# Block two's recurrent mixer in another order: convolution and gate products before the dense gate branch, its functions grouped over all heads

## The reference, cut to what matters

```
def recurrent_mixer(h, ...):
    gate_branch = gelu(h @ w_y + b_y)
    xr = h @ w_in + b_in
    xr = causal_depthwise_conv_2(xr, conv_w, conv_b)       # width 4
    gate_r = sigmoid(block_diag(xr, w_a) + b_a)            # 4 heads of 256 x 256
    gate_i = sigmoid(block_diag(xr, w_x) + b_x)
    log_a = 8.0 * gate_r * log_sigmoid(lam)
    a, mult = exp(log_a), sqrt(-expm1(2.0 * log_a))
    h_t = a_t * h_{t-1} + mult_t * gate_i_t * xr_t         # over the 512 tokens
    return (h * gate_branch) @ w_out + b_out
```

## Time and profile before

| what | value |
|---|---|
| median of 3 runs | 2665.47 us (2664.84 to 2668.5) |
| the profiled execution | 2664.44 us |
| its span, first to last instruction | 2662.4 us |
| granted TensorE clock, mean | 0.942 |
| PE busy | 2396.6 us, 90% |
| DVE busy | 1375.9 us, 52% |
| ACT busy | 1017.8 us, 38% |

### The profile page before, as it was taken

One profiled execution on the slowest core, in us unless ns is written; L12 is line 12 of the kernel. 1 busy time (PEld: TensorE's weight loads), 2 busy tenths in 40 slices (PEclk: granted clock), 3 DMA queues, 4 the chain that ended last, 5 costly groups with the idle time before them and its releaser, 6 DMA issues.

```text
span 2662.4 us, 35555 instructions
## 1 busy us (share of the span) xinstructions
PE 2396.6 (90%) x13228; PEld 1916.8 (72%) x13228; DVE 1375.9 (52%) x1960; ACT 1017.8 (38%) x1543; POOL 308.6 (12%) x250
## 2 busy tenths in 40 slices
PE   8996689999999996689999997948999993799998
PEld 6774567888877774667888886736888883688886
DVE  3546656656544546655656544545443345434433
ACT  5534334323234544324423235374332233423323
POOL 0032312000031032312000021011000013100001
PEclk9998699999999999699999998978999996899999
DMA  4210003555432210003555431211222221122222
GB/s 153 72 63 9 2 27 126 195 184 196 135 111 68 75 60 12 2 18 118 194 189 193 144 105 54 87 40 64 95 95 95 95 95 39 48 95 95 95 95 87
DMA packets 68648, 247.68 MB, mean 93 GB/s; under 512 B 7616, under 2 KB 8128, under 8 KB 68544
## 3 DMA queue, kind: packets, MB, share of 16 engines
q1 hardware_dynamic: 68544, 246.26, 27.8%
HBM read 244.13 MB, written 2.10 MB: 92 GB/s over the span
## 4 chain that ended last, share of the span: by engine, by line
PE 79%; DVE 10%; ACT 5%; issue 3%; POOL 1%; DMA 0%; SPq 0%; DVEq 0%; ACTq 0%; POOLq 0%
PE dense L532 23%; PE dense L533 22%; PE dense L534 22%; PE aux L769 1%; PE aux L630 1%; DVE outer L1987 1%; DVE inv L1989 1%; PE aux L937 1%; PE aux L740 1%; PE aux L756 1%; PE aux L637 1%; ACT wh L1146 1%; DVE nt L1758 1%; PE aux L532 1%; PE aux L747 1%
## 5 line engine op out<-in xcount | busy, mean ns | idle before, releaser
L532 PE MATMUL dense<-xh,wh 128*128 128x512 f32 x1904 | 757.1, 398 | 52.3 <-DVE xl L1732 25.6
L1146 ACT ACTIVATE wh<-raw 128x1024 fp32r<-128x1024 f32 x342 | 362.4, 1060 | 1030.3 <-PE dense L534 1016.5
L533 PE MATMUL dense<-xl,wh 128*128 128x512 f32 x1904 | 745.8, 392 | 0.0
L534 PE MATMUL dense<-xh,wl 128*128 128x512 f32 x1904 | 745.2, 391 | 0.0
L1700 DVE TENSOR_TENSOR wl<-raw,wh 128x1024 fp32r<-128x1024 f32 x342 | 419.1, 1225 | 573.7 <-ACT wh L1146 572.2
L532 PEld LDWEIGHTS dense<-xh,wh 128*128 128x128 f32 x1904 | 360.2, 189 | 152.9 <-DVE xl L1732 39.9
L534 PEld LDWEIGHTS dense<-xh,wl 128*128 128x128 f32 x1904 | 359.9, 189 | 76.5
L533 PEld LDWEIGHTS dense<-xl,wh 128*128 128x128 f32 x1904 | 360.1, 189 | 73.8 <-issue 1.7
L532 PE MATMUL dense<-hidh,wh 128*128 128x512 f32 x864 | 342.4, 396 | 1.9 <-DVE hidl L1732 1.9
L534 PE MATMUL dense<-hidh,wl 128*128 128x512 f32 x864 | 341.7, 396 | 0.0
L533 PE MATMUL dense<-hidl,wh 128*128 128x512 f32 x864 | 341.7, 395 | 0.0
(11 more groups left out here) (328 smaller groups left out, 2482.5 us busy)
## 6 DMA issues: line engine op xcount, KB each, us to landing
raw<-stream SPq DMA_DIRECT2D x362, 512.0 KB, 3.3
mraw<-mod_stream SPq DMA_DIRECT2D x96, 512.0 KB, 4.2
x<-x_t SPq DMA_DIRECT2D x4, 512.0 KB, 7.4
y_t<-x SPq DMA_DIRECT2D x8, 256.0 KB, 2.1
cst<-consts SPq DMA_DIRECT2D x1, 993.0 KB, 10.3
cond<-c_rows SPq DMA_DIRECT2D x1, 512.0 KB, 11.5
pv_next<-vecs SPq DMA_DIRECT2D x3, 82.5 KB, 4.5
pv<-vecs SPq DMA_DIRECT2D x1, 116.0 KB, 10.7
```

The source lines that it names most:

```text
L532: pe.matmul(o, a, h, start=first, stop=False)
L533: pe.matmul(o, a, l, start=False, stop=False)
L534: return pe.matmul(o, b, h, start=False, stop=last)
L1146: act.activation(wh[:, slot].rearrange("p k m -> p (k m)"), raw[:, slot, :], ACT.Copy).then_inc(hi_done, 1)
```

## The change

The stream's order becomes C_IN (8), C_AX (4), C_Y (8), C_OUT (8).

- PE: `arriving` runs over C_IN; the head products use all six `aux` banks in turn, and the n-th of the 16 outputs waits only for the sigmoid of output n - 6; then C_Y; then C_OUT from `hidh` and `hidl` in place of `xh` and `xl`, so that `xh`, `xl` keep the mixer's input for C_Y.
- ACT: conv inputs as before, then all sigmoids and tanh of the four heads, then the 8 exp with the 8 squares, the 8 square roots, the 8 gelus with the rounding of the 8 outputs. The conversions of C_Y's and C_OUT's chunks stand at fixed places between them.
- DVE: for C_Y's first four chunks it copies the raw bank to `gate` (`gate_raw`), and Gelu is done later in place; the rest of the gates come from the bank. Scans of tile m, the product with the gate, and the low part follow, with the chunk conversions between them.
- `ga`, `gx` and `tb` hold all eight tiles, in buffers that are free then.

The rest (counts of semaphores shifted by 8, `triple` and `paired` that take their operands as arguments) follows from these. The core of the diff:

```
-C_Y, C_IN, C_AX, C_OUT, C_F0 = 0, 8, 16, 20, 28
+C_IN, C_AX, C_Y, C_OUT, C_F0 = 0, 8, 12, 20, 28
...
             norm_sums(4)
-            arriving(pl, C_Y, 6, 16, in_turn(xl_ready, XL2))
+            arriving(pl, C_IN, 6, KT, in_turn(xl_ready, XL2))
             for h in range(4):
                 pe.wait_ge(lo_done, pl.chunk(C_AX + h) + 1)
                 pe.wait_ge(hidl_ready, H0 + 2 * h + 2)
-                if h:
-                    pe.wait_ge(ax_read, 4 * h)
                 for o in range(4):
+                    n = 4 * h + o
+                    if n >= 6:
+                        pe.wait_ge(ax_read, n - 5)
                     for k in range(2):
-                        m = split_product(aux[o][:], (h % 2, (2 * o + k) * P), slice(0, P),
+                        m = split_product(aux[n % 6][:], (h % 2, (2 * o + k) * P), slice(0, P),
                                           (hidh[:, 2 * h + k, :], hidl[:, 2 * h + k, :]),
                                           k == 0, k == 1)
-                m.then_inc(pe_chunk, 1)
-            arriving(pl, C_OUT, 7, KT, in_turn(xl_ready, XL2 + 8))
+                    m.then_inc(pe_chunk if o == 3 else ax_pe, 1)
+            section(pl, C_Y, KT, xh, xl)
+            arriving(pl, C_OUT, 7, KT, in_turn(hidl_ready, H0 + 8), range(KT), hidh, hidl)
...
+            def gates(h):
+                for o in range(4):
+                    m, to = 2 * h + o % 2, (ga, gx)[o // 2]
+                    if o < 3:
+                        act.wait_ge(ax_pe, 3 * h + o + 1)
                     else:
+                        done(pl, C_AX + h)
+                    act.activation(to[m], aux[(4 * h + o) % 6][:], ACT.Sigmoid,
+                                   bias=vec2(("b_a", "b_x")[o // 2], m)).then_inc(ax_read, 1)
+            def tanhs(h):
+                act.wait_ge(ax_read, 4 * h + 2)
+                for m in (2 * h, 2 * h + 1):
+                    act.activation(tb[m], ga[m], ACT.Tanh, scale=small[:, 7, m:m + 1])\
+                       .then_inc(th_ready, 1)
...
+            for h in range(4):
                 gates(h)
+                tanhs(h)
+            for m in range(4):
+                decays(m)
+                if m:
+                    decay_square(m - 1)
+            done(pl, C_Y)
+            for m in range(4, KT):
+                decays(m)
+                decay_square(m - 1)
+            decay_square(KT - 1)
+            done(pl, C_Y + 1)
+            for m in range(KT):
+                root(m)
+            done(pl, C_Y, 1)
+            gelu(0)
+            gelu(1)
+            done(pl, C_Y + 1, 1)
+            gelu(2)
+            gelu(3)
+            for m in range(4, KT):
+                done(pl, C_Y + m % 2, m // 2)
+                gelu(m)
+                if m < 7:
+                    gated_hi_2(2 * (m - 4))
+                    gated_hi_2(2 * (m - 4) + 1)
+            gated_hi_2(6)
+            gated_hi_2(7)
...
+            def gate_raw(m):
+                i, j = m // 2, m % 2
+                dve.wait_ge(pe_chunk, pl.chunk(C_Y + j, i) + 1)
+                dve.tensor_copy(gate[:, m, :], dbank[j][:]).then_inc(bank_free[j], 1)
+                refill(pl, C_Y + j, i)
...
+            for m in range(3):
+                one_minus_a2(m)
+            gate_raw(0)
+            for m in range(3, KT):
+                one_minus_a2(m)
+            gate_raw(1)
+            for m in range(2):
+                scan(m)
+            gate_raw(2)
+            for m in range(2, 4):
+                scan(m)
+            gate_raw(3)
+            for m in range(4, KT):
+                scan(m)
+                if m == 5:
+                    refill(pl, C_Y, 2)
+                    gated(0)
+                    gated(1)
+            refill(pl, C_Y + 1, 2)
+            gated(2)
+            gated(3)
+            gated_lo(0)
+            gated_lo(1)
+            refill(pl, C_Y, 3)
+            gated(4)
+            gated(5)
+            gated_lo(2)
+            gated_lo(3)
+            refill(pl, C_Y + 1, 3)
+            gated(6)
+            gated(7)
+            for m in range(4, KT):
+                gated_lo(m)
```

More of the change, by code:

```diff
@@ L547, in dense, with triple @@
                 m.then_inc(pe_chunk, 1)
[L549 removed]
+            def triple(s, k, h=xh, l=xl):
                 slot = s % 2
@@ L575, in shared_low, with paired @@
                 return wait
-            def paired(pl, s, q, tile, order):
+            def paired(pl, s, q, tile, order, h=xh, l=xl):
                 done = []
@@ L1534, in _, with conv_input @@
             modulated(4, lambda m: small[:, 4, m:m + 1], lambda m: mod[:, 0, m:m + 1])
-            early(pl, C_Y, 6)
-            for i in range(4):
-                for j in range(2):
-                    m = i * 2 + j
-                    if i == 0:
-                        rest(pl, C_Y + j)
-                    else:
-                        done(pl, C_Y + j, i)
+            def conv_input(i, j):
+                m = i * 2 + j
+                act.wait_ge(xc_ready, m)
+                act.wait_ge(ua_zero, DEPTH + 1)
+                act.activation(ua[:, 3:S + 3], dbank[j][:], ACT.Identity,
+                               bias=vec2("b_in", m)).then_inc(bank_free[j], 1)
+                act.wait_ge(xc_ready, m + 1)
+                act.activation(hidh[:, m, :], xc[:, m, :], ACT.Copy).then_inc(hidh_ready, 1)
@@ new lines, in root, with gelu @@
+            def root(m):
+                act.wait_ge(m2_ready, m + 1)
+                act.activation(tb[m], tb[m], ACT.Sqrt).then_inc(m_ready, 1)
+            def gelu(m):
+                i, j = m // 2, m % 2
+                if m < 4:
+                    act.wait_ge(bank_free[j], pl.use(C_Y + j, i) + 1)
+                    act.activation(gate[:, m, :], gate[:, m, :], ACT.Gelu_apprx_tanh,
+                                   bias=vec2("b_y", m)).then_inc(gate_ready, 1)
+                else:
@@ L1543, in _ @@
                     act.activation(gate[:, m, :], dbank[j][:], ACT.Gelu_apprx_tanh,
                                    bias=vec2("b_y", m)).then_inc(bank_free[j], 1)
[L1545 to L1593, removed]
-                gates(h)
-                roots(h - 1)
@@ L1596, in _, with gated_hi_2 @@
-            roots(3)
+            def gated_hi_2(m):
+                act.wait_ge(h_ready, m + 1)
+                act.activation(hidh[:, m, :], xc[:, m, :], ACT.Copy).then_inc(hidh_ready, 1)
+            for h in range(4):
+                gates(h)
+                tanhs(h)
[7 more added lines that the diff above has]
+                decay_square(m - 1)
@@ L2196, in _ @@
             for j in range(2):
-                rest(pl, C_Y + j)
-            with dve.Fori(1, 4) as i:
+                rest(pl, C_IN + j)
+                conv(0, j)
+            with chain.loop(3, 6) as i:
                 for j in range(2):
[L2200 to L2213, removed]
-                    dve.wait_ge(hidh_ready, H0 + m + 1)
-                    low(hidl[:, m, :], xc[:, m, :], hidh[:, m, :], hidl_ready)
@@ L2240, in _, with one_minus_a2 @@
-            one_minus_a2(0)
-            for h in range(1, 4):
-                one_minus_a2(h)
-                scan(h - 1)
-            scan(3)
+                    refill(pl, C_IN + j, i + 1)
+                    conv(i + 1, j)
+            for h in range(4):
+                refill(pl, C_AX + h)
+            def one_minus_a2(m):
+                dve.wait_ge(th_ready, m + 1)
+                dve.wait_ge(a2_ready, m + 1)
+                stt(tb[m], nt[:, m % 2, :], 1.0, tb[m], ADD, MUL).then_inc(m2_ready, 1)
@@ new lines, in gated, with gated_lo @@
+            def gated(m):
+                if m < 4:
+                    dve.wait_ge(gate_ready, m + 1)
+                else:
+                    dve.wait_ge(bank_free[m % 2], pl.use(C_Y + m % 2, m // 2) + 1)
+                tt(xc[:, m, :], xc[:, m, :], gate[:, m, :], MUL).then_inc(h_ready, 1)
+            def gated_lo(m):
+                dve.wait_ge(hidh_ready, H0 + 8 + m + 1)
+                low(hidl[:, m, :], xc[:, m, :], hidh[:, m, :], hidl_ready)
+            for m in range(3):
+                one_minus_a2(m)
```

102 lines of the change are left out of this document (61 added, 41 removed).

## The result

| | before | after |
|---|---|---|
| median of the runs on one chip | 2665.22 us (2664.84 to 2668.5) | 2624.94 us (2623.42 to 2629.36) |
| the profiled execution | 2664.44 us | 2623.42 us |
| its span | 2662.4 us | 2621.3 us |
| granted TensorE clock, mean | 0.942 | 0.949 |

Ratio 0.9849, 95% interval [0.9832, 0.9866]. The forecast was 2622.0 with a range of 2616 to 2632: the time lies in it, 2.9 us above the forecast.

The account below looks back on a forecast made before the run. The prediction took PE's matmul stream as the bound, with idle and half-clock time in the mixer to win. Its steps moved the third C_OUT chunk from 1811.05 to 1767.5, gaining 43.5 us: 2665.47 - 43.5 = 2622.0, range 2616 to 2632.

Parts of the forecast that it names:

- step 1: Mixer's convolution: first two rounds 5 us each, later ones 6.13 us per tile, last `hidh` at 1690.0.
- step 2: Head products: PE idles 3 us, seventh output starts at 1692.6, head 2 waits 0.6 us, end at 1707.2.
- cold stretch in the head products: Rival: the 3 us of idling take the clock down, costing 2.4 us, to 2624.5; chance 15%.
- step 3: C_Y beside the grouped functions: 43.5 us of chunks plus 2.6 us of waits, end at 1753.3.
- DVE nearly full: Sign in C_Y: DVE's load is 41.8 of 46 us, `wl` ending at or under 1 us after PE's previous chunk.
- DVE becomes the bound: Rival in C_Y: DVE steps 10% longer add 4 us, 20% some 8, giving 2626 to 2630; chance 18%.
- step 4: C_OUT: second chunk waits 2.1 us, 15 triples take 10.5, end 1766.6, third chunk at 1767.5.
- the mark: Mixer time from the first pair's end to the third C_OUT chunk: 166.3 us before, forecast 121 to 125.
- From there on everything is as before: From the third C_OUT chunk on, nothing changes; the next norm's square-root table load follows ACT's last square, within its wait.
- if that cover were gone: Next norm: the square root's table load would cost 1.3 us if not hidden in ACT's wait for the sums.
- The grouping doesn't hold: Rival in C_Y: alternating functions need 8 to 12 loads of 1.29, 10 to 15 us back, 2632 to 2637; chance 2%.
- slower than before: Rival: short PE idles hold the clock at 1.2 GHz, 20 chunks each 4.8 us longer, 2718; chance 2%.

Follow-up runs that it names:

- e7_by_head: Kernel after, with exp, square and root done head by head as before, six banks kept, Y2 and Y3 conversions after heads 1 and 3; 2636.82 us.
- e3_sig_early: Kernel after, with the sigmoid's table loaded before the column products of C_IN, outside PE's wait for the first sigmoid; 2620.21 us.
- e9_group_only: Kernel after's grouped functions and six banks, but in the old stream order C_Y, C_IN, C_AX, C_OUT; 2652.32 us.
- e5_fill: Kernel after, with one useless float32 identity matmul in PE's wait before the seventh head output; 2624.91 us.
- e2_before_align: Kernel before, with `hidh`, `hidl` and every buffer behind them moved up by 32 bytes; 2649.85 us.
- e8_dve_more: Kernel after, with one added DVE product of 0.60 us behind each of the eight scans; 2631.74 us.
- e1_align: Kernel after, with `hidh`, `hidl` and every buffer behind them moved up by 32 bytes; 2611.25 us.
- e6_four_banks: Kernel after, with head products in four banks, each head waiting for all sigmoids of the head before; 2634.51 us.
- e4_sqrt_early: Kernel after, with the square root's table loaded directly behind the last square of C_OUT; 2623.1 us.
- e10_best: Kernel after, with rows moved to a multiple of 64 bytes and the sigmoid's and square root's tables loaded early; 2606.57 us.

## Why the prediction was right, step by step

**Convolution (step 1).** Right: the last `hidh` was forecast at 1690.0, and starts at 1689.98. The first two rounds taken at 5 us each held.

**Head products (step 2).** The seventh output was forecast at 1692.6 after 3 us of idling; it starts at 1692.66 after 2.86. The end came at 1708.31, not 1707.2. This is the term that was mis-sized: I took no fall of the clock after 3 us because 2.12 us had shown none, and it did fall, for eight steps of 0.38 to 0.43 instead of 0.233: 1.5 us of the 2.4 that stood as the bound. Part of it came back, as head 2 did not wait the 0.6 us assumed. The rival "cold stretch in the head products" was thus real. `e7_by_head` and `e3_sig_early`, whose clock stays up here, give its net price: from the seventh output to the next dense chunk they take 14.66 and 14.67 us, with 0.30 of waiting before head 2, and the kernel after 15.65, so 1.0 us. The runs show that it isn't settled by the length of the wait alone: after 2.86 us the clock stayed up in `e7_by_head`, after 2.87 in the head products of `e9_group_only`, and it fell after 2.00 in `e5_fill`. The row I leaned on was no firm ground either: the same wait before C_Y's third chunk, now 2.13 us, is followed by eight half-clock steps in `e9_group_only` and in `e2_before_align`.

**C_Y (step 3).** It lasts 1754.43 - 1708.31 = 46.1 us, and 46.1 were forecast (43.5 of chunks, 2.6 of waits). The single waits were not where I put them: those that the trace shows are 0.39 us at most, the rest is in the restarts behind them. "DVE nearly full" was too strong as a busy share: the window gives 37.7 of 46.1 us, 82%, since the last two gate products and most of the last six low parts fall behind C_Y's end. As a statement about order it held, and `e8_dve_more` is its proof: 0.60 us more behind each scan came through with 4.5 of 4.8 as waits. The rival "DVE becomes the bound" had its mechanism right, and did not happen, as its steps were not longer than in the rows.

**C_OUT (step 4).** 1768.61 - 1754.43 = 14.2 us, as forecast (1767.5 - 1753.3); the wait was 1.78, forecast 2.1. So the mark stands 1.1 us late, all of it from step 2: 123.8 for 122.7, within the 121 to 125 given.

**"From there on everything is as before"** failed twice, by small terms. The first is the pace of the six remaining C_OUT chunks: I had changed their operands in my list, from `xh`, `xl` to `hidh`, `hidl`, but not their price. The steps of 0.2333 us of the head products were in the earlier trace rows, and I used them for the triples and not for the rest: 6 x (5.60 - 5.44) = 1.0 us, which `e1_align` gives back by moving the rows. The second is the table load for the norm's square root: I had it "right after ACT's last square, in its wait for the sums"; it stands behind that wait (idle 1.49 us ahead of 1807.14). The four earlier loads of the same line (at 419.65, 799.61, 1224.13 and 1603.50 us) do follow the last square at once and run in the wait, so the expectation was not baseless; why this one doesn't is open. The row sums follow 3.21 us after the column sums, where the kernel before took 2.63 with no load there. That difference of 0.6 is two things: the 1.3 us priced for "if that cover were gone" came in full, as PE's wait before the row sums went from 0.76 to 2.04 us, and 0.7 us of it was hidden by luck, as the column sums took 1.16 us where the kernel before took 1.87 at a granted clock of 0.50. `e6_four_banks` has both, the load outside the cover and column sums of 1.87, and needs 3.91 us. With the load in the cover the step takes 1.81 in `e4_sqrt_early` (column sums 1.05) and 2.63 in `e10_best` (1.86).

The sum: 43.5 - 1.1 - 1.0 - 0.6 = 40.8; the two profiled executions differ by 41.0. That it closes so well is luck too. It needs both executions to reach the end of the first pair at the same time, and they do (1644.76 and 1644.77); in the kernels e4 to e9, whose work up to that point is the same, it comes between 1643.15 and 1647.65.

**Table loads.** In C_Y and the head products there are four, and the next activation follows each by 1.29 to 1.30 us (1690.62 to 1691.92). The Trainium skill, "ScalarE: Activation LUTs", section "What ACT_TABLE_LOAD costs", adds about 1380 ns of drain to each switch; no load of the mixer shows it, before or after. In the whole trace of the kernel after, the next activation comes within 1.31 us of 16 of the 23 loads, and the other seven stand ahead of a wait for DVE or a DMA. "The grouping doesn't hold" and "slower than before" did not occur: four loads in place of the twelve that the mixer had before, and a clock of 1.00 in C_Y.

**Why the large change gave what it promised.** It removed no matmul, only table loads and waiting. `e9_group_only` shows that grouping (with six banks) alone gives 11 to 13 us, because the chain of exp, root, scan and gate then leaves PE idle for 29 us (21.32 and, over the six tiles after it, 7.6) with nothing left to multiply beside it; the chunks of C_Y are that work, and DVE's lists just fit beside them.

## What to carry to other kernels

When an engine waits in several places for a long chain of others, look for products that depend on none of it and lay them beside the whole chain; grouping the chain alone only gathers the waits in one. When a product is given other operands, take its price from rows with those operands, down to their address. And say of each table load on which side of the neighbouring wait it stands: name its place with an explicit load.

## What the runs showed of the hardware

- A 128x512 matmul whose moving operand starts at 32 bytes past a multiple of 64 has a pace of 0.2333 us, at a multiple of 64 of 0.2267. One line of padding moved both kernels by 14 us (0.9944 and 0.9794 of before). The Trainium skill, "SBUF — State Buffer", section "Operand start alignment", allows any multiple of the element's size and says that its runs timed nothing; here is a price for a legal address. Of the 14 us the traces attribute the pace of these matmuls; what the other buffers behind that line, which it moves too, add or take was not separated.
- The clock can fall after idles of 1.77 to 2.87 us, and need not: eight slow steps after 2.86 in the kernel after, twelve after 2.87 in `e1_align`, none after 2.86 in `e7_by_head`; eight after 2.13 in `e9_group_only` and `e2_before_align`, none after 2.12 in the kernel before, at the same place; eight after 1.77 or 1.78 in `e5_fill`, `e4_sqrt_early` and `e8_dve_more`, none after 1.78 in the kernel after, at the same place. In `e6_four_banks` two waits of 1.87 us stand 8 us apart, and only the second is followed by slow steps, eight of them. Why one and not the other is open; no run here separates it.
- On which side of a wait a table load stands, if no line of the kernel asks for it, can't be taken for granted. Of the five loads for the norms' square roots (line 1196) in the kernel after, four run in the wait, and the one at 1807.14 stands behind it: 1.49 us idle, then 1.28 of load. An explicit load ahead of the wait (`e4_sqrt_early`) ran in it, and PE's wait for the row sums fell from 2.04 to 0.76 us.
